# A trunk layer with a top-2 expert stage on one core: other order of the first loads, the first unit's weight homes freed by halves, the last unit's second matrices and its adding store by column halves

## The chip, the core and the metric

The kernel runs on one core of a Trainium2 chip. The time is the device time of the core in microseconds. Three runs of the kernel before took 1055.2, 1055.73 and 1056.48 us. Everything is float32.

## What is computed

One inference step of one trunk layer on 640 tokens (512 latent, 128 context) of width 1024:

```
mod = silu(cond) @ w_ada + b_ada                  # 6 x 1024 shifts, scales, gates; two conditions
h   = rmsnorm(x) * (1 + sc1) + sh1
x   = x + g1 * token_mixing(h)                    # Fourier, RG-LRU, short convolution, attention, merged by gates
h   = rmsnorm(x) * (1 + sc2) + sh2
x   = x + g2 * moe(h)                             # 32 experts, top-1 group of 8, top-2 in it
expert e: y = (silu(h @ w1[e]) * (h @ w3[e]) * weight) @ w2[e]     # 1024 -> 256 -> 1024
```

The change touches the very start (the first modulation chunks) and the expert stage.

## The kernel before

Each engine has its own instruction list, in an order written out by hand; semaphores tie them together. All loads of weights are issued by SyncE (the SP queue), one after another in that list, and land in about that order. GpSimd (POOL) issues the indirect transfers.

**Start.** `w_ada` comes in 12 chunks of 2 MB (`ada0` to `ada11`). TensorE turns each into a row of modulations (`modulation`, L812), ScalarE copies it out (`take_rows`, L1443), `modulation_T` (L823) turns two rows into columns, and VectorE makes shifts and scales of them (L1786 to L1802). Beside it the tokens `x0` (1.5 MB, three tiles) and `x1` (1 MB, two tiles) are squared on ScalarE (L1440), POOL makes the inverse norms, and VectorE scales the tokens (L1779). VectorE first waits for `consts` (the identity among them, L1768), since its list has that wait ahead of L1779. TensorE then transposes the tokens (`tokens_T`, L829), ScalarE and VectorE modulate them on their way out of PSUM (L1448, L1794), and the first input projection `zP0` (L867) begins; it also needs `win0`. Only chunks 0 and 2 are needed for that. `spin(n, 3)` (L835) issues n products of a block of ones whose result nobody reads; it stands ahead of chunk 0 (48) and between chunks 0 and 2 (14).

**Expert stage.** 17 units (0 to LAST = 16) of two experts each (unit 8 has one, for tokens beyond an expert's 64 rows). An expert's matrices are one block: W1 and W3 together (`w13`, 2 MB) and W2 (`w2`, 1 MB). There are NBUF = 6 homes, so that expert i+6 takes the home of expert i. For a unit u TensorE's list is: transpose its 128 gathered rows (`pair_T`, L1321), `hidden_of(u)` (L1328: 32 products over 8 blocks of rows, in two halves, and between them the transpose of the unit before), and `project` (L1344: 16 products). The order in the loop is `hidden_of(u+1)`, `pair_T(u+2)`, `project(u)`. When `hidden_of(u)` is done (`s_A`), SP issues the `w13` of the two experts that follow in those homes; when `project(u)` is done (`s_Y`), their `w2`. ScalarE and VectorE make the activation and, after the unit before has been scaled (`s_yd`), the gate rows for this one (`slot_g2`: L1706 on ScalarE, then L2395 on VectorE). VectorE multiplies the product with them, 512 columns at a time (L2405), and POOL adds the 128 rows to the output in HBM by one indirect transfer (`scatter`, L2632). POOL also gathers the rows of the units (L2628).

**Around unit 0** TensorE's list is: `second_gate_row(0)` (L1369), `hidden_of(0)`, `second_gate_row(1)`, `pair_T(1)`, the table of left-over tokens (L1382, 20 products into the same PSUM slot as the gate rows), then the loop, which begins with `hidden_of(1)`. ScalarE takes out of PSUM, in this order: the rows of unit 0 (L1683), both gate rows (L1693), the rows of unit 1.

**The last unit** has experts 31 and 32 of the stream. Before, SP issues their `w13` as the two lower halves, then the two upper halves (`w13_rest`), so that TensorE can begin on the lower halves; their `w2` comes last, whole.

Of the kernel before, what the change touches and what calls it, by code (L numbers as in the profile page):

```python
# [15 lines left out]
KD = D // P  # L16
# [145 lines left out]
W13_PIECES = [4 if 2 <= i < NBUF else 1 for i in range(len(STREAM))]  # L162
# [31 lines left out]
def build(nc, a, out):  # L194
    ctx = ExitStack()
    with ctx:
# [3 lines left out]
        def sem(name):  # L200
            return ctx.enter_context(nc.semaphore(name))
# [135 lines left out]
        xtab = sb("xtab", 3, I32)  # L337

# [128 lines left out]
        s_first = sem("first_unit_rows_chosen")  # L467
# [23 lines left out]
        w13_rest = sem("last_w13_upper_rows_loaded")  # L491
# [102 lines left out]
        def _(sp):  # L594
# [18 lines left out]
            load("cols", cols[:, :], a["cols"])  # L613
            load("x0", xtok[:, 0:3, :], x_dram[:, 0:3, :])
            load("x1", xtok[:, 3:TT, :], x_dram[:, 3:TT, :])
            ring("ada0", a["w_ada"][0])
            load("consts", consts[:, :], a["consts"])
            ring("ada2", a["w_ada"][2])
# [72 lines left out]

            for e in range(2):
                load_w13(e)
                load_w2(e)
# [53 lines left out]
            for u in range(LAST + 1):  # L748
                if u == 2:

                    sp.wait_ge(s_xtab, 2)
                    for h in range(2):
                        sp.dma_start(table_d[0:2 * XCOLS].rearrange("(c h) r k -> h r c k", h=2)[h], tab[h * C:(h + 1) * C, PAIRS:TCOLS, :]) \
                            .then_inc(s_over, 16)
                    sp.wait_ge(s_slot, 1)
                    e_x = sp.value_load(xinfo[0:1, 0:1], min_val=0, max_val=NE - 1)
                    n_x = sp.value_load(xinfo[0:1, XCH:XCH + 1], min_val=1, max_val=XCH)
                if AFTER[u]:
                    sp.wait_ge(s_A, u + 1)
                for i in AFTER[u]:  # L760
                    if i in AT[LAST]:
                        load_piece(i, wexp[i % NBUF][0][:, 0:W13 // 2], 0, W13 // 2, w13_loaded[i % NBUF])
                    else:
                        load_w13(i)
                for i in AFTER[u]:
                    if i in AT[LAST]:
                        load_piece(i, wexp[i % NBUF][0][:, W13 // 2:W13], W13 // 2, W13, w13_rest)
                if u and AFTER[u - 1]:
                    sp.wait_ge(s_Y, u)
                    for i in AFTER[u - 1]:  # L770
                        load_w2(i)
# [11 lines left out]
            sp.wait_ge(y_stored[0], 16 * (LAST // 2 + 1))  # L783
# [6 lines left out]
        def _(pe):  # L790
# [47 lines left out]
            spin(48, 3)  # L838
            pe.wait_ge(s_scond, 1)
            modulation(0)  # L840
            spin(14, 3)
# [496 lines left out]
            def project(halves, slot=2):  # L1338

                for n in range(2):  # L1340
                    for f in range(2):
                        for lo, homes, hid in halves:
                            w = homes[f] if len(homes) == 2 else homes[0][:, f * D:(f + 1) * D]
                            ins = mm(psum[lo:lo + C, slot, n * 512:(n + 1) * 512], hid[:, f, :],  # L1344
                                     w[:, n * 512:(n + 1) * 512], start=(f == 0), stop=(f == 1))
                return ins
# [5 lines left out]
            def hidden_of(u):  # L1352
                for i in AT[u]:
                    pe.wait_ge(w13_loaded[i % NBUF], 16 * pieces_until(W13_PIECES, i))
                pe.wait_ge(s_xTd, u + 1)
                halves = [(lo, wexp[i % NBUF][0], xgT[u % 2][:, :, lo:lo + C]) for lo, i in zip((0, C), AT[u])]
                hidden(H_SLOT[u % 2], halves, range(0, KD // 2))
                if u:
                    pe.wait_ge(s_hid, u)
                    hidden_T(H_SLOT[(u - 1) % 2], gate_e[:, (u - 1) % 2, :]).then_inc(s_hf, 1)  # L1360
                if u == LAST:
                    pe.wait_ge(w13_rest, 16 * len(AT[LAST]))
                hidden(H_SLOT[u % 2], halves, range(KD // 2, KD)).then_inc(s_A, 1)
# [7 lines left out]

            pe.wait_ge(s_lgd, TT)
            second_gate_row(0)
            pe.wait_ge(s_cntd, 2)
            hidden_of(0)
            pe.wait_ge(s_g2r, 1)
            second_gate_row(1)
            pair_T(1)
# [6 lines left out]
            for u in range(LAST + 1):  # L1385
# [10 lines left out]
                if u and u < LAST:  # L1396
                    pe.wait_ge(s_yd, u)
                pe.wait_ge(s_hT, u + 1)
                project([(lo, wexp[i % NBUF][1:], hT[:, u % 2, :, lo:lo + C]) for lo, i in zip((0, C), AT[u])], Y_SLOT[u]) \
                    .then_inc(s_Y, 1)  # L1400
# [24 lines left out]
        def _(act):  # L1425
# [265 lines left out]
            for i in range(2):  # L1691
                act.wait_ge(s_g2f, i + 1)
                A(g2_row[:, i, :], psum[:, 2, :], ACT.Copy).then_inc(s_g2r, 1)  # L1693
            take_pair_T(1)
            act.wait_ge(s_g2r, 2)
# [31 lines left out]
        def _(dve):  # L1727
# [603 lines left out]
            v.tensor_copy(pair_w[:, 0:PAIRS, :], filled_tab[:, :, 1:3]).then_inc(s_tab, 1)  # L2331

# [56 lines left out]
            for p in range(LAST + 1):  # L2389
# [14 lines left out]
                for n in range(2):  # L2404
                    ins = v.tensor_tensor(y_sb[:, p % 2, n * 512:(n + 1) * 512],  # L2405
                                          psum[:, Y_SLOT[p], n * 512:(n + 1) * 512], slot_g2[n], ALU.mult)
                ins.then_inc(s_yd, 1)
# [38 lines left out]
        def _(pool):  # L2446
# [191 lines left out]
            def put_rows(u):  # L2638
# [9 lines left out]
                scatter(y_sb[0:n, u % 2, :], tab[0:n, TAB_COL[u], 0:1], y_stored[u % 2])  # L2648
# [145 lines left out]
```

## Time and profile before

| | |
|---|---|
| median of three runs | 1055.73 us (1055.2 to 1056.48) |
| the profiled execution, its own time | 1053.14 us |
| its span from first to last instruction | 1051.3 us |
| PE, DVE, ACT, POOL busy | 94%, 49%, 22%, 25% of the span |
| mean granted TensorE clock | 0.977 of full |
| moved by DMA | 193.65 MB, 184 GB/s over the span |

A time stamp counts from the span's start. A busy share says how much an engine worked, not that it set the end: for that the chain of waits is read back from the last instruction, and in the expert stage the rate of the transfers in short windows.

### The profile page before, as it was taken

The numbers are of one execution on the slowest core, as the hardware profiler recorded it, in microseconds if no ns is written. First come the engines' busy times: TensorE is split into PE (matmuls) and PEld (weight loads), VectorE is DVE, ScalarE is ACT, GpSimd is POOL, SyncE is SP. The second block draws the span as 40 slices with busy tenths as digits, with TensorE's granted clock in tenths as the row PEclk, the third lists the DMA queues.
The fourth block names the chain that finished last, engine by engine and source line by source line (L and its number), as shares of the span: only waits on it lengthen the run. The fifth ranks groups of instructions, "written<-read, shape, count | busy, mean of one in ns | idle before, by whom it ended". The sixth has DMA issues, their size and how long they took to land.

```text
span 1051.3 us, 11753 instructions
## 1 busy us (share of the span) xinstructions
PE 992.0 (94%) x4332; PEld 590.7 (56%) x4332; DVE 516.0 (49%) x1018; ACT 232.9 (22%) x464; POOL 265.0 (25%) x268
## 2 busy tenths in 40 slices
PE   8899999999999999999999999999999998878785
PEld 6566656655555677777777777745584332322231
DVE  3378652255645345667667655537674321321223
ACT  3224330134555311111111111111112111211111
POOL 0333310011530133544465334200010211211101
PEclk9999999999999999999999999999989998998988
DMA  9735346000000271221311421275379999999995
GB/s 370 298 139 230 120 177 254 1 6 2 1 1 1 101 289 52 65 87 51 101 51 57 166 68 61 79 274 168 113 292 355 332 401 398 399 426 399 403 409 175
DMA packets 37625, 193.65 MB, mean 184 GB/s; under 512 B 7658, under 2 KB 12458, under 8 KB 27712
## 3 DMA queue, kind: packets, MB, share of 16 engines
q1 hardware_dynamic: 32800, 182.31, 45.1%
q0 software_dynamic: 4624, 10.06, 3.9%
q8 instruction: 35, 0.57, 0.2%
q10 hardware_dynamic: 144, 0.52, 0.1%
q14 instruction: 22, 0.18, 0.1%
HBM read 185.50 MB, written 14.09 MB: 190 GB/s over the span
## 4 chain that ended last, share of the span: by engine, by line
PE 79%; DMA 10%; SPq 3%; DVE 2%; issue 2%; ACT 2%; POOL 0%; POOLq 0%; DVEq 0%; ACTq 0%
PE psum L1110 23%; PE psum L867 8%; PE psum L1144 7%; PE psum L1186 7%; PE psum L1328 6%; DMA r_bv<-in_w_e 4%; PE psum L960 3%; PE psum L1344 3%; DMA r_w<-in_w_e 3%; PE psum L1044 3%; SPq L678 2%; PE psum L1060 2%; PE psum L812 2%; DMA r_w<-in_w_ada 2%; PE psum L1071 2%
## 5 line engine op out<-in xcount | busy, mean ns | idle before, releaser
L1110 PE MATMUL psum<-r_h,r_w 128*128 128x320 f32 x512 | 143.6, 433 | 0.0
L2604 POOL TENSOR_TENSOR r_w<-r_w 128x512 f32<-128x512 f32 x64 | 84.7, 1332 | 221.6 <-PE psum L1110 155.0
L1110 PEld LDWEIGHTS psum<-r_h,r_w 128*128 128x128 f32 x512 | 97.1, 190 | 40.6 <-issue 0.3
L1110 PE MATMUL psum<-r_ys,r_w 128*128 128x320 f32 x384 | 111.2, 432 | 0.0
L1110 PEld LDWEIGHTS psum<-r_ys,r_w 128*128 128x128 f32 x384 | 73.0, 190 | 30.4
L1613 ACT ACTIVATE r_bv<-r_bv 128x320 f32<-128x320 f32 x64 | 30.1, 470 | 238.8 <-DVE r_bv L2141 238.8
L2632 POOL DMA_INDIRECT out_y<-r_bv,tab x17 | 26.8, 1577 | 202.0 <-DVE r_bv L2405 202.0
L1186 PE MATMUL psum<-r_w,r_bv 128*128 128x512 f32 x160 | 72.2, 597 | 0.0
L2150 DVE TENSOR_TENSOR r_t<-psum,r_t 128x320 f32<-128x320 f32 x112 | 52.2, 483 | 9.3 <-PE psum L1144 8.0
L2127 DVE SCALAR_TENSOR_TENSOR r_t<-r_bv,r_t 128x320 f32<-128x320 f32 x48 | 46.8, 975 | 1.2 <-ACT r_bv L1613 1.2
L2141 DVE TENSOR_TENSOR sqbuf<-psum,r_bv 128x320 f32<-128x320 f32 x32 | 15.7, 492 | 64.4 <-PE psum L1110 64.4
L1687 ACT ACTIVATE r_t<-psum 128x256 f32<-128x256 f32 x17 | 6.5, 385 | 182.1 <-PE psum L1328 180.2
L1186 PEld LDWEIGHTS psum<-r_w,r_bv 128*128 128x128 f32 x160 | 29.2, 190 | 30.3 <-issue 30.3
L2385 DVE COPY r_t<-psum 128x256 f32<-128x256 f32 x17 | 7.2, 425 | 77.5 <-PE psum L1335 77.5
L2085 DVE TENSOR_REDUCE tinys<-psum 128x1 f32<-128x640 f32 (+1 forms) x40 | 28.6, 716 | 18.5 <-PE psum L1045 18.3
L1044 PE MATMUL psum<-r_a,r_bv 96*128 96x512 f32 x64 | 34.5, 620 | 2.5 <-ACT r_bv L1552 0.8
L2141 DVE TENSOR_TENSOR r_bv<-psum,r_bv 128x320 f32<-128x320 f32 x32 | 15.7, 491 | 41.8 <-PE psum L1110 41.7
L2136 DVE TENSOR_TENSOR r_bv<-r_bv,r_t 128x320 f32<-128x320 f32 x48 | 35.8, 746 | 0.4
L2378 DVE SCALAR_TENSOR_TENSOR r_t<-r_t,psum 128x256 f32<-128x256 f32 x17 | 7.2, 421 | 58.0 <-ACT r_t L1687 58.0
L1328 PE MATMUL psum<-r_c,r_ckv 128*64 128x512 f32 x64 | 30.3, 620 | 4.9 <-issue 4.9
L2454 POOL TENSOR_TENSOR tinys<-tinys 128x2 f32<-128x2 f32 (+2 forms) x11 | 7.6, 690 | 105.6 <-DVE tinys L2202 105.1
L2395 DVE SCALAR_TENSOR_TENSOR sqbuf<-r_d,tab,sqbuf 128x512 f32<-128x512 f32 x17 | 12.8, 751 | 35.0 <-ACT r_d L1706 35.0
(461 smaller groups left out, 2019.0 us busy)
## 6 DMA issues: line engine op xcount, KB each, us to landing
r_a<-in_w_ada SPq DMA_DIRECT2D x8, 2048.0 KB, 8.5
r_w<-in_w_gate SPq DMA_DIRECT2D x32, 512.0 KB, 4.6
r_a<-in_w_e SPq DMA_DIRECT2D x6, 2048.0 KB, 31.7
r_c<-in_w_e SPq DMA_DIRECT2D x5, 2048.0 KB, 31.2
r_c<-in_w_e SPq DMA_DIRECT2D x8, 1024.0 KB, 34.9
r_w<-in_w_e SPq DMA_DIRECT2D x4, 2048.0 KB, 34.3
r_ys<-in_w_e SPq DMA_DIRECT2D x4, 2048.0 KB, 36.4
r_bv<-in_w_e SPq DMA_DIRECT2D x4, 2048.0 KB, 36.6
```

Source lines behind the costliest of these rows:

```text
L867: ins = mm(dst, w_n[:, k, :], z_mix0[:, k // 2, k % 2, :] if n == 4 else x[:, k, :], start=(k == 0), stop=(k == HK - 1))
L960: mm(o[:, 0:512], x, w[:, 0:512], start=(k == 0), stop=(k == KD - 1))
L1044: mm(o[:, 0:NLAT], q, kT[0:QK, h, 0:NLAT], start=True, stop=True)
L1110: ins = mm(gate_bank(u, n), w[:, k, :], x[:, k, :], start=(k == 0), stop=(k == HK - 1))
L1144: ins = mm(branch_bank(u, seq), x_w[:, k, :], xs_[k], start=(k == 0), stop=(k == kb - 1))
L1186: ins = mm(out_bank(t, n), merged[:, k, tokens_of(t)], w[:, (k % 4) * D + n * 512:(k % 4) * D + (n + 1) * 512], start=(k == 0), stop=(k == ...
L1328: ins = mm(psum[lo:lo + C, slot, 0:2 * FE], xT[:, k, :], w[:, k * 2 * FE:(k + 1) * 2 * FE], start=(k == 0), stop=(k == KD - 1))
L1344: ins = mm(psum[lo:lo + C, slot, n * 512:(n + 1) * 512], hid[:, f, :], w[:, n * 512:(n + 1) * 512], start=(f == 0), stop=(f == 1))
L2127: v.scalar_tensor_tensor(out=merged[:, 2 * i + j, part] if b == 0 else bquad[n], in0=gth[:, j, part], scalar=1.0, in1=bquad[n], op0=ALU.ad ...
L2136: v.tensor_tensor(merged[:, 2 * i + j, part], merged[:, 2 * i + j, part], bquad[n], ALU.add) \
L2150: v.tensor_tensor(bsum[:, dst, :], branch_bank(u, seq), bsum[:, more, :], ALU.add).then_inc(s_badd, 1)
L2604: g.tensor_tensor(w_mix[n], x, y, op).then_inc(s_wm, 1)
```

## The change

Start: `ada0` is issued ahead of the tokens, and `ada2` ahead of `consts`. The products of ones are 22 ahead of chunk 0 and 44 between chunks 0 and 2.

Unit 0: its two homes are reloaded in halves. `s_first` counts once more when the lower half of `hidden_of(0)` is done; SP then issues the lower halves of experts 6 and 7, and the upper halves after `s_A`. In TensorE's list `hidden_of(0)` stands ahead of `second_gate_row(0)`, and `pair_T(1)` ahead of `second_gate_row(1)`; ScalarE's list follows.

Last unit: `w13` comes whole again. Its `w2` comes as 512 left columns of both experts, then 512 right columns. `project`, the scaling and the adding store go by these halves: two indirect stores of 128 rows x 512 columns, with row numbers `last_rows` of an output seen as 1280 rows of 512.

```diff
-W13_PIECES = [4 if 2 <= i < NBUF else 1 for i in range(len(STREAM))]
+W13_PIECES = [4 if 2 <= i < NBUF else 2 if i in (NBUF, NBUF + 1) else 1 for i in range(len(STREAM))]
...
+            ring("ada0", a["w_ada"][0])
             load("x0", xtok[:, 0:3, :], x_dram[:, 0:3, :])
             load("x1", xtok[:, 3:TT, :], x_dram[:, 3:TT, :])
-            ring("ada0", a["w_ada"][0])
+            ring("ada2", a["w_ada"][2])
             load("consts", consts[:, :], a["consts"])
-            ring("ada2", a["w_ada"][2])
             ring("win0", a["w_in"][0])
...
+            def load_w2_columns(i, n, done):
+                halves = lambda w: w.rearrange("p (f n) -> p f n", f=2)[:, :, n * 512:(n + 1) * 512]
+                sp.dma_start(halves(wexp[i % NBUF][1]), halves(a["w_e"][STREAM[i][1], :, W13:EW])).then_inc(done, 16)
...
+                if u == 0:
+                    sp.wait_ge(s_first, TT + 1)
+                    for i in AFTER[0]:
+                        load_w13(i, (0,))
                 if AFTER[u]:
                     sp.wait_ge(s_A, u + 1)
                 for i in AFTER[u]:
-                    if i in AT[LAST]:
-                        load_piece(i, wexp[i % NBUF][0][:, 0:W13 // 2], 0, W13 // 2, w13_loaded[i % NBUF])
+                    if u == 0:
+                        load_w13(i, (1,))
                     else:
                         load_w13(i)
-                for i in AFTER[u]:
-                    if i in AT[LAST]:
-                        load_piece(i, wexp[i % NBUF][0][:, W13 // 2:W13], W13 // 2, W13, w13_rest)
                 if u and AFTER[u - 1]:
                     sp.wait_ge(s_Y, u)
                     for i in AFTER[u - 1]:
-                        load_w2(i)
+                        if i not in AT[LAST]:
+                            load_w2(i)
+                    for n, done in enumerate((w2_loaded, [w2_rest] * NBUF)):
+                        for i in AFTER[u - 1]:
+                            if i in AT[LAST]:
+                                load_w2_columns(i, n, done[i % NBUF])
...
             pe.wait_ge(s_set, 1)
-            spin(48, 3)
+            spin(22, 3)
             pe.wait_ge(s_scond, 1)
             modulation(0)
-            spin(14, 3)
+            spin(44, 3)
             modulation(2)
...
-                hidden(H_SLOT[u % 2], halves, range(0, KD // 2))
+                ins = hidden(H_SLOT[u % 2], halves, range(0, KD // 2))
+                if u == 0:
+                    ins.then_inc(s_first, 1)
...
+            pe.wait_ge(s_cntd, 2)
+            hidden_of(0)
             pe.wait_ge(s_lgd, TT)
             second_gate_row(0)
-            pe.wait_ge(s_cntd, 2)
-            hidden_of(0)
+            pair_T(1)
             pe.wait_ge(s_g2r, 1)
             second_gate_row(1)
-            pair_T(1)
...
+                else:
+                    project(halves, Y_SLOT[u], (0,)).then_inc(s_Y, 1)
+                    pe.wait_ge(w2_rest, 16 * len(AT[LAST]))
+                    project(halves, Y_SLOT[u], (1,)).then_inc(s_Y, 1)
...
-            for i in range(2):
+            def take_second_gate_row(i):
                 act.wait_ge(s_g2f, i + 1)
                 A(g2_row[:, i, :], psum[:, 2, :], ACT.Copy).then_inc(s_g2r, 1)
+            take_second_gate_row(0)
             take_pair_T(1)
+            take_second_gate_row(1)
...
+            for h in range(2):
+                v.tensor_scalar(last_rows[:, h:h + 1], filled_tab[:, TAB_COL[LAST], 0:1], 2.0, h - 2.0, ALU.mult, ALU.add)
...
+                half_rows = out["y"].rearrange("t (h n) -> (t h) n", h=2)
+                for h in range(2):
+                    pool.wait_ge(s_yd, u + 1 + h)
+                    pool.indirect_dma_start(half_rows, bass.IndirectOffsetOnAxis(ap=last_rows[:, h:h + 1], axis=0),
+                                            y_sb[:, u % 2, h * 512:(h + 1) * 512], None, bounds_check=2 * NT - 1,
+                                            oob_is_err=False, compute_op=ALU.add).then_inc(y_stored[u % 2], 16)
```

## Rows read from the trace of the kernel before

**Rows 1.** Page, DMA busy share in tenths, 40 slices of 26.3 us.

```profile
DMA  9735346000000271221311421275379999999995
```

**Rows 2.** Chain that ended last, the start: start us, us, what.

```profile
3.81 19.45 DMA r_w<-in_w_ada
...
32.06 4.54 PE psum L867 x16
```

**Rows 3.** Timeline, the start: start us, us, engine, line [idle before <- releaser].

```profile
1.44 13.30 PE L835 MATMUL psum<-ones 128*128 128x128 f32 x96 [1.44 <-DVE ones L1732]
...
16.11 1.92 PE L812 MATMUL psum<-r_w,scond 128*32 128x512 f32 x16 [1.37 <-DMA r_w<-in_w_ada]
...
17.38 0.08 DVE L1768 MEMSET tinys<- 128x30 f32 x1 [8.69 <-DMA consts<-in_consts]
...
17.83 3.39 DVE L1779 TENSOR_SCALAR r_a<-r_a,tinys 128x1024 f32<-128x1024 f32 x5
...
17.96 3.39 PE L835 MATMUL psum<-ones 128*128 128x128 f32 x28
...
23.30 3.61 PE L812 MATMUL psum<-r_w,scond 128*32 128x512 f32 x16 [1.95 <-DMA r_w<-in_w_ada]
...
28.23 2.50 POOL L2482 TENSOR_TENSOR r_a<-r_ys 128x512 f32<-128x512 f32 x2 [12.01 <-DMA r_ys<-in_w_in]
...
28.59 2.35 PE L829 MATMUL psum<-consts,r_a 128*128 128x128 f32 x20
...
29.57 1.18 DVE L1802 SCALAR_TENSOR_TENSOR mod<-ada,cols 128x8 f32<-128x8 f32 x1
```

**Rows 4.** Windows, the start: us, busy of each engine (count), TensorE clock, DMA share, GB/s.

```profile
23.40:26.80 3.40, 3.40 (x16) 0.49 (x15) 0.00 (x0) 0.00 (x0) 0.00 (x0) 0.50 1.04 443
```

**Rows 5.** Windows of the expert stage.

```profile
794.00:797.00 3.00, 3.00 (x24) 2.30 (x21) 0.83 (x2) 0.34 (x1) 0.00 (x0) 1.00 0.72 213
...
806.00:810.00 4.00, 4.00 (x24) 1.64 (x22) 0.84 (x2) 1.57 (x3) 0.00 (x0) 1.00 0.51 140
...
836.00:1033.00 197.00, 165.65 (x708) 58.48 (x706) 49.80 (x88) 31.52 (x48) 31.88 (x24) 0.92 1.02 405
```

**Rows 6.** Chain that ended last, TensorE around unit 0.

```profile
785.65 1.98 PE psum L1369 x16
787.63 7.02 PE psum L1328 x32
...
797.83 2.39 PE psum L1382 x20
```

**Rows 7.** Timeline around unit 0: ScalarE's copy, SP's issue.

```profile
785.63 1.02 ACT L1683 ACTIVATE r_ckv<-psum 128x1024 f32<-128x1024 f32 x1 [8.70 <-PE psum L1233]
...
807.80 0.33 SPq L678 DMA_DIRECT2D r_w<-in_w_e  x1
```

**Rows 8.** Chain that ended last, the end.

```profile
1038.30 3.67 PE psum L1344 x16
```

**Rows 9.** DMA issued at 991.99 us (last w13 piece): KB, us to landing.

```profile
r_w<-in_w_e SPq DMA_DIRECT2D x1, 1024.0 KB, 35.1
```

**Rows 10.** Timeline, the end.

```profile
1025.65 0.59 PE L1328 MATMUL psum<-r_c,r_ckv 128*64 128x512 f32 x1
...
1038.30 0.61 PE L1344 MATMUL psum<-r_c,r_t 128*64 128x512 f32 x1 [1.29 <-DMA r_w<-in_w_e]
...
1038.80 0.72 ACT L1706 ACTIVATE sqbuf<-r_d,tab 128x512 f32<-128x512 f32 x1 [3.94 <-DVE r_bv L2405]
...
1040.84 0.74 DVE L2395 SCALAR_TENSOR_TENSOR r_d<-r_d,tab 128x512 f32<-128x512 f32 x1
...
1042.66 0.68 DVE L2405 TENSOR_TENSOR r_bv<-psum,r_d 128x512 f32<-128x512 f32 x1
...
1044.13 1.55 POOL L2632 DMA_INDIRECT out_y<-r_bv,tab  x1 [3.02 <-DVE r_bv L2405]
```

**Rows 11.** DMA issued at 1044.13 us (last adding store): us to landing.

```profile
out_y<-r_bv,tab POOLq DMA_INDIRECT x1, 5.6
```

More of the change, by code:

```diff
@@ L337, in build @@
         xtab = sb("xtab", 3, I32)
+        last_rows = sb("last_rows", 2, I32)
         R = {}
@@ L466, in build @@
         s_h2d = sem("h2_stored")
-        s_first = sem("first_unit_rows_chosen")
+        s_first = sem("first_unit_rows_chosen_and_low_half_projected")
         s_g2f, s_g2r = sem("second_gate_rows_filled"), sem("second_gate_rows_ready")
@@ L490, in build @@
         w13_loaded = [sem(f"w13_loaded{i}") for i in range(NBUF)]
-        w13_rest = sem("last_w13_upper_rows_loaded")
+        w2_rest = sem("last_w2_upper_columns_loaded")
         w2_loaded = [sem(f"w2_loaded{i}") for i in range(NBUF)]
@@ L782, in _ @@
             overflow(sp, n_x, load_chunk)
-            sp.wait_ge(y_stored[0], 16 * (LAST // 2 + 1))
+            sp.wait_ge(y_stored[0], 16 * (LAST // 2 + 2))
             sp.wait_ge(y_stored[1], 16 * (LAST // 2))
@@ L1336, in hidden_T, with project @@
                 return ins
-            def project(halves, slot=2):
-                for n in range(2):
+            def project(halves, slot=2, ns=range(2)):
+                for n in ns:
                     for f in range(2):
@@ L1360, in hidden_of @@
                     hidden_T(H_SLOT[(u - 1) % 2], gate_e[:, (u - 1) % 2, :]).then_inc(s_hf, 1)
-                if u == LAST:
-                    pe.wait_ge(w13_rest, 16 * len(AT[LAST]))
                 hidden(H_SLOT[u % 2], halves, range(KD // 2, KD)).then_inc(s_A, 1)
@@ L1398, in _ @@
                 pe.wait_ge(s_hT, u + 1)
-                project([(lo, wexp[i % NBUF][1:], hT[:, u % 2, :, lo:lo + C]) for lo, i in zip((0, C), AT[u])], Y_SLOT[u]) \
-                    .then_inc(s_Y, 1)
+                halves = [(lo, wexp[i % NBUF][1:], hT[:, u % 2, :, lo:lo + C]) for lo, i in zip((0, C), AT[u])]
+                if u < LAST:
+                    project(halves, Y_SLOT[u]).then_inc(s_Y, 1)
+                else:
+                    project(halves, Y_SLOT[u], (0,)).then_inc(s_Y, 1)
+                    pe.wait_ge(w2_rest, 16 * len(AT[LAST]))
+                    project(halves, Y_SLOT[u], (1,)).then_inc(s_Y, 1)
                 if u == 2:
@@ L2404, in _ @@
                 for n in range(2):
+                    if p == LAST:
+                        dve.wait_ge(s_Y, p + 1 + n)
                     ins = v.tensor_tensor(y_sb[:, p % 2, n * 512:(n + 1) * 512],
                                           psum[:, Y_SLOT[p], n * 512:(n + 1) * 512], slot_g2[n], ALU.mult)
-                ins.then_inc(s_yd, 1)
+                    if n or p == LAST:
+                        ins.then_inc(s_yd, 1)
                 if p != LAST - 2:
@@ L2647, in put_rows @@
                 n = rows_of(u)
-                scatter(y_sb[0:n, u % 2, :], tab[0:n, TAB_COL[u], 0:1], y_stored[u % 2])
+                if u < LAST:
+                    scatter(y_sb[0:n, u % 2, :], tab[0:n, TAB_COL[u], 0:1], y_stored[u % 2])
+                    return
+                half_rows = out["y"].rearrange("t (h n) -> (t h) n", h=2)
[4 more added lines that the diff above has]
+                                            oob_is_err=False, compute_op=ALU.add).then_inc(y_stored[u % 2], 16)
             pool.wait_ge(s_wo, 2 * TT)
```

## The prediction

> **What bounds the kernel now.** I read the digits of the DMA share first: high in the first slices, low through the middle, 9 to the end from slice 30 on [rows 1]. So three regimes: a start fed by loads, a long middle with few transfers, and an expert stage with full transfers. Then the chain of waits, start and end, tells which wait ends last in each.
>
> Start: the chain is the landing of `ada2` at 23.26 (3.81 + 19.45), its product, the column transposes, the modulation of the tokens, and `zP0` at 32.06 [rows 2]. The timeline shows the loads landing in issue order: `ada0` at 16.1, `consts` at 17.4, `ada2` at 23.3, `win0` at 28.2, and that the tokens are scaled (L1779) from 17.83, right after `consts`, long before they are wanted at 28.59 [rows 3]. The product of chunk 2 runs at the low clock, 0.50 granted or 1.2 GHz, and takes 3.61 us instead of 1.92 [rows 3, 4].
>
> Expert stage: from 836 to 1033 the DMA share is 1.02 at 405 GB/s while TensorE is busy 165.65 of 197 us [rows 5]. TensorE waits for weights, not weights for TensorE. The stream has two holes ahead of that: 794 to 797 (213 GB/s) and 806 to 810 (140 GB/s) [rows 5]. Against 405 that is 3 x 192 / 405 = 1.4 us and 4 x 265 / 405 = 2.6 us of lost transfer. The first is the wait for unit 0's homes, the second ends with the reload issued at 807.80, which is the end of `hidden_of(1)` [rows 7]. End: last `w2` landed just before 1038.30, 16 products until 1041.97, scaling until 1043.34, store issued at 1044.13 and landed 5.6 later at 1049.7 [rows 8, 10, 11].
>
> **Part 1, the start.** No byte is added. `ada0` gets ahead of 2.5 MB of tokens; at 4.9 us per 2 MB (`ada2` to `win0`, 28.2 - 23.3) it lands 6.1 us earlier, at 10.0. `ada2` gets ahead of `consts` (17.4 - 16.1 = 1.3 us): 22.0. `consts` closes the same sum of bytes as `ada2` did: 23.3. `win0` stays at 28.2 [rows 3].
> The products of ones: the first 48 took 13.30 us (slow at first), the next 14 took 3.39, or 0.24 each; so 22 end near 9, and 44 after chunk 0's product (10.0 + 1.9 = 11.9) take some 10 and end at 22. The product of chunk 2 then runs without an idle gap at the high clock until 23.9, and ScalarE's copy and the column transposes (before: from 26.91 to 28.59, 1.7 us) are done at 25.6. That is 3.0 us earlier than before.
> But `consts` is now late: VectorE's list goes from 17.38 to 23.3, and the scaled tokens come at 23.3 + 0.45 + 3.39 = 27.2 instead of 21.2 [rows 3]. The token transposes wait for all five: 27.2 instead of 28.59. VectorE's shifts and scales are queued behind the tokens in its own list. Before, the last of these small operations took 1.18 us, beside POOL's mixing of `win0` (28.23 to 30.7) [rows 3]; now they come ahead of it and are estimated at 0.6 together, so done at 27.8, in time for the first transposed block. Four blocks of transposes take 2.35, so `zP0` starts at 29.6, after `win0` (28.2). Gain 32.06 - 29.6 = **2.4 us**. What follows is TensorE's own chain, and the next loads are not earlier but had room; so the gain is kept until the expert stage.
> Bounds: up to 3.0, if only the modulation chain counts; 1.4, if the small operations stay as long (27.2 + 32.06 - 28.59 = 30.7); down to 0.9, if the idle gap of 1.6 us between the column and the token transposes costs the high clock. The trace has a gap of 1.37 us after which the product took 1.92, and one of 1.95 after which it took 3.61 [rows 3, 4]. I take the first, as the nearer one; the second is a stretch of 3.4 us at half speed, of which about 1.5 lie on the path (the rest under the wait for VectorE).
>
> **Part 2, unit 0.** SP issues two lower halves once half of `hidden_of(0)` is done. That list is TensorE's, so the order counts. Before: gate row 1.98, hidden 7.02 (until 794.65), gate row again 1.98, 1.2 until the table, filled by `pair_T(1)` (1.1), table 2.39, `hidden_of(1)` at 800.22 [rows 6]. After:
> - `hidden_of(0)` needs ScalarE's copy of its rows, 785.63 to 786.65; the first gate row covered that. It now starts at 786.7 and ends at 793.7, 0.9 earlier; its half is done at 790.2.
> - gate row 0 until 795.7; ScalarE copies it (1.0) under `pair_T(1)`, until 796.8.
> - gate row 1 until 798.8. `pair_T(1)` used to cover its copy. Now nothing does: ScalarE is done at 799.9.
> - table until 802.3. `hidden_of(1)` starts **2.1 us later** than before, and so do its end (809.9), the issue of experts 8 and 9, and the restart of the stream.
> The lower halves are in the queue at 790.3, the older loads last until 794.6, so the first hole is filled: 1.4 us. But the 4 MB then end at about 805, and the second hole reaches from there until the reload after `hidden_of(1)`. Since nothing is left in the queue then, all later bytes start 2.1 us later, behind a stream that is full until 1033. Cost **+2.1 us**. Bounds: if the restart were not what counts, the filled hole would give -1.4; if the new idle times of 1.1 us (785.6 and 798.8) took the clock down, one stretch of 3.4 us at half speed as in [rows 4] adds up to 1.7: +3.8.
>
> **Part 3, the last unit.** The bytes are the same, the last piece lands at 1038.2 as before (relative to the stream). What changes is who waits for what:
> - `hidden_of(LAST)` started at 1025.65 on the lower halves [rows 10]; the upper half of expert 32 landed at 991.99 + 35.1 = 1027.1 [rows 9]. Now both whole blocks are needed at the start: TensorE begins up to 1.4 us later.
> - TensorE before stood 1.29 us idle ahead of the last product, so its delay is hidden there. But the gate rows are not: ScalarE begins them when the unit before is scaled, 1038.80, and VectorE is done with them at 1041.6 [rows 10], 0.4 ahead of the product's end. 1.4 later they are ready at 1043.0, and VectorE's two halves end at 1043.7 and 1044.4 (before: 1043.34 the second).
> - POOL issues two stores, 1.55 each and some 0.3 between. First at 1043.7 + 0.8 = 1044.5, second at 1046.3 instead of 1044.13 [rows 10]. Half the rows' bytes are left for it: landing after 5.6 if the size does not matter, after 2.8 if it all does [rows 11]. I take 4.6, since the 1.55 of issue come first in it and do not shrink. It lands at 1050.9 instead of 1049.7: **+1.2 us**.
> Bounds: -0.8 (no delay of `hidden_of(LAST)`, second store landing in 4.0), +2.3 (size of the store without effect).
> The Trainium skill bears on this place: "DMA: Bandwidth & Descriptors", section "Anatomy of one DMA", gives a transfer issued by GpSimd about 2 us fixed and the rest as bytes over 436 GB/s, so that halving a store of 0.5 MB would save an estimated 0.6 us. By it alone the second store lands in 5.0 and the part costs 1.6. It speaks against splitting a store whose issue is serial.
> `last_rows` adds two small VectorE operations beside idle time; the `w2` column halves are 2 KB runs instead of 8 KB, taken at nothing (up to 0.4).
>
> **Sum.** -2.4 + 2.1 + 1.2 = +0.9 on the profiled 1053.14 (1051.3 and 1.8 around it): 1054.0. The median of the runs is 2.6 above the profiled one; the forecast for the median is 1055.73 + 0.9 = **1056.6 us**.
>
> **Rivals.**
> - A, the forecast, +0.9. Chance 0.42.
> - B, the filled hole counts and the later restart does not. For it: TensorE is idle 31 us of the 197 later on [rows 5], so its lateness at one unit might drown. Against: the queue is empty at the restart. -2.4 - 1.4 + 1.2 = -2.6, 1053.1 us. Chance 0.28.
> - C, slower: the start's new idle gap of 1.6 us ahead of the token transposes takes the clock down, place L829 and `zP0`, price 1.5 of the 2.4. It decides from a gap between 1.37 (kept) and 1.95 (lost). +0.9 + 1.5 = +2.4, 1058.1 us. Chance 0.20.
> - D, the new order of loads does not do what it says, since `consts` or chunk 0 lands later than worked out and the chain is no shorter than before: +3.3, 1059.0 us. Chance 0.10.
>
> What a measurement of this kernel can tell from no change is 0.2%, 2.1 us: below 1053.6 is faster, above 1057.8 slower. B lies just below, C just above, A in the middle. Faster: most of B and an edge of A, 0.25. Slower: most of C, D, 0.23. Same 0.52. The range that holds 8 in 10 goes from half a microsecond beyond B to half one beyond C: 1052.5 to 1058.7; A's own is 1054.8 to 1058.
>
> **What would show it.** Start: L812's second group at 22 and 1.92 long; L1768 at 23.3; L829 near 27.2; `zP0` near 29.6. Unit 0: ScalarE's second L1693 ends right ahead of L1382; `hidden_of(1)` 2 us later against the end of L1233; 794 to 797 at full rate, and a longer hole until the reload of experts 8 and 9. End: first L1328 of the last unit waits for r_w; the two L2632 stand 1.8 apart, and the second lands under 5.6. I am wrong if the span from the reload of experts 8 and 9 to the last `w2` landing gets shorter by more than 1 us, or if the holes of 794 to 810 lose less than 4 us in all.

## The result, and the profile after

The changed kernel takes 1062.66 us (median of 5, 1060.67 to 1064.47) beside 1055.20 for the kernel before on the same chip: ratio 1.0065, 95% interval [1.0045, 1.0085]. It is 6.9 us slower, where 0.9 was forecast, and outside the range given. The profiled execution took 1063.33 us with a span of 1061.3; before it was 1053.14 with 1051.3, an execution 2.1 to 2.6 below its medians. So the two profiles lie 10.0 apart and the medians 7.5.

In the changed kernel `hidden` is L1339, the gate rows L1380, the table L1393, `pair_T` L1332, `project` L1355. The chain of waits around unit 0 (start us, us, what) answers to [rows 6]:

```profile
785.94 1.03 ACT r_ckv L1699
...
787.10 7.09 PE psum L1339 x32
794.19 1.99 PE psum L1380 x16
...
796.21 1.03 ACT r_d L1709
...
797.28 2.06 PE psum L1380 x16
...
799.37 1.03 ACT r_d L1709
...
800.54 3.15 PE psum L1393 x20
803.69 6.13 PE psum L1339 x16
...
810.19 3.58 PE psum L1339 x16
```

The order is as worked out: second gate row, ScalarE's copy on the path, table. But the table takes 3.15 instead of 2.39, and the first 16 products of `hidden_of(1)` take 6.13 where the next 16 of the same form take 3.58. The windows of the expert stage (us, busy of PE, PEld, DVE, ACT, POOL with counts, TensorE clock, DMA share, GB/s) say why:

```profile
794.00:797.00 3.00, 3.00 (x26) 2.72 (x24) 1.14 (x2) 0.79 (x1) 0.00 (x0) 1.00 1.05 423
802.00:808.80 6.80, 6.80 (x23) 3.02 (x24) 1.10 (x4) 0.38 (x1) 0.00 (x0) 0.50 0.54 223
806.00:810.00 4.00, 4.00 (x14) 1.04 (x10) 0.00 (x0) 0.00 (x0) 0.00 (x0) 0.65 0.02 10
810.00:814.00 4.00, 4.00 (x21) 1.36 (x20) 0.42 (x1) 0.18 (x1) 0.00 (x0) 1.00 0.00 0
...
1034.00:1037.50 3.50, 3.50 (x10) 1.29 (x12) 0.00 (x0) 0.00 (x0) 1.03 (x1) 0.51 1.03 402
```

The clock stood at 0.50, 1.2 GHz, for 6.8 us of uninterrupted products. What TensorE did before it fell is in the timeline. It stood idle under ScalarE's copies, 1.14 us ahead of `hidden_of(0)` and 1.21 us ahead of the table:

```profile
787.10 0.61 PE L1339 MATMUL psum<-r_a,r_ckv 128*64 128x512 f32 x1 [1.14 <-ACT r_ckv L1699]
...
800.54 3.15 PE L1393 MATMUL psum<-r_bv,r_t 128*128 128x30 f32 x20 [1.21 <-ACT r_d L1709]
```

The clock fell at 802.0, 1.5 us after the second of them had ended and 14.9 after the first. The first hole of the stream is filled (423 GB/s, before 213 [rows 5]), the second is 8 us of nearly nothing (10 and 0 GB/s). It ends with the reload of experts 8 and 9:

```profile
790.79 0.33 SPq L679 DMA_DIRECT2D r_a<-in_w_e  x1
...
813.81 0.33 SPq L679 DMA_DIRECT2D r_w<-in_w_e  x1
```

That is 6.0 later than before [rows 7]. The start, in the chain:

```profile
4.46 18.71 DMA consts<-in_consts
...
23.77 3.33 DVE r_a L1798 x5
...
27.14 4.04 PE psum L840 x20
31.18 4.31 PE psum L878 x16
```

`zP0` (L878) starts 0.9 earlier than at 32.06 [rows 2]. The end, in the timeline:

```profile
1033.95 0.98 PE L1339 MATMUL psum<-r_c,r_ckv 128*64 128x512 f32 x1 [2.86 <-issue]
...
1048.84 0.72 ACT L1725 ACTIVATE sqbuf<-r_d,tab 128x512 f32<-128x512 f32 x1 [3.94 <-DVE r_bv L2428]
...
1053.72 1.55 POOL L2678 DMA_INDIRECT out_y<-r_bv,last_rows  x1 [2.56 <-DVE r_bv L2428]
1055.58 1.55 POOL L2678 DMA_INDIRECT out_y<-r_bv,last_rows  x1 [0.30 <-issue]
```

DMAs issued at 1027.85 (the last piece of `w2`) and at 1055.58 (the second store), us to landing:

```profile
r_w<-in_w_e SPq DMA_DIRECT2D x1, 512.0 KB, 17.3
...
out_y<-r_bv,last_rows POOLq DMA_INDIRECT x1, 4.0
```

The last weight is there at 1045.2, the last store at 1059.6. Before, [rows 8, 11] put them at 1038.2 and 1049.7: the tail grew from 11.5 to 14.4 us.

**The account.** Four lengths between events that every trace shows, in us. Stage: SP's first issue of the expert stage. Reload: from there to the issue of experts 8 and 9. Stream: from there to the last landing of `w2`. Late: from there until ScalarE begins the last gate rows, which is when unit 15 has been scaled. Chain: from there to the landing of the last store.

| kernel | stage | reload | stream | late | chain |
|---|---|---|---|---|---|
| before | 768.0 | 39.8 | 230.4 | 0.6 | 10.9 |
| changed | 768.3 | 45.5 | 231.4 | 3.7 | 10.8 |
| e1 start only | 766.6 | 38.9 | 230.1 | 0.1 | 11.3 |
| e2 unit 0 only | 768.1 | 45.5 | 230.6 | 0.0 | 11.2 |
| e3 last only | 768.1 | 40.4 | 230.4 | 3.7 | 11.0 |
| e4 unit 0, filled | 768.3 | 42.2 | 230.1 | 0.0 | 12.9 |
| e5 halves only | 769.9 | 38.9 | 231.0 | 2.7 | 10.3 |
| e6 order only | 765.5 | 44.6 | 231.2 | 2.7 | 10.3 |
| e7 whole w13 only | 768.6 | 39.9 | 230.6 | 3.6 | 10.4 |
| e8 unit 1 first | 767.4 | 35.8 | 233.3 | 0.1 | 11.2 |
| e9 last, filled | 766.8 | 39.8 | 230.5 | 2.0 | 10.9 |
| e10 last, w13 by halves | 765.5 | 39.9 | 230.6 | 2.4 | 10.8 |
| e11 start, filled | 767.8 | 38.9 | 230.8 | 2.4 | 10.2 |
| e12 all, filled | 767.0 | 41.3 | 230.8 | 2.2 | 10.8 |
| e13 unit 1 first + start | 766.7 | 35.8 | 231.2 | 2.4 | 10.3 |

Of the 9.9 us between the two profiles, 0.3 lie ahead of the stage, 5.7 in unit 0, 1.0 in the stream and 2.9 in the tail. The table also warns of what one execution is worth. Kernels with an unchanged start reach the stage at 765.5 to 769.9. With an unchanged last unit the tail (late and chain) is 11.2 to 11.5 four times (before, e1, e2, e8) and 12.7 to 13.0 five times (e4, e5, e6, e11, e13), and these five are the ones in which the clock fell to 0.50 for 3.4 us while the last two units' products ran (at 1028.5 to 1041.0).

The reload column holds 0.9 us of such chance too. In all fifteen profiles the clock falls once between 768 and 776 us, ahead of unit 0, for 6.8 us in eight of them and for 3.4 in seven, and from the stage's first issue to SP's issue of the two loads into `r_bv` (785.59 in the kernel before, 785.89 in the changed one) it takes 17.6 to 18.2 us in the eight and 16.7 in the seven. Counted from that issue, the reload depends on the order and the fillers alone, to 0.02 us:

| TensorE's order around unit 0 | kernels | us to the reload |
|---|---|---|
| as before | before, e1, e3, e5, e7, e9, e10, e11 | 22.2 |
| the change's, idle times open | changed, e2, e6 | 27.9 |
| the change's, idle times filled | e4, e12 | 24.6 |
| unit 1 ahead of the table | e8, e13 | 19.1 |

### The profile page after: what moved, and what is told of

The parts are those of the page before. It is cut to its first block, busy times and chain, and to the rows that moved or that the text cites. A ratio compares the mean times of both kernels' runs of the same rounds, so it can differ in the third digit from the quotient of the medians.

```text
span 1061.3 us, 11776 instructions
## 1 busy us (share of the span) xinstructions
PE 999.3 (94%) x4340; PEld 596.9 (56%) x4340; DVE 515.0 (49%) x1020; ACT 232.8 (22%) x464; POOL 266.3 (25%) x269
## 3 DMA queue, kind: packets, MB, share of 16 engines
q1 hardware_dynamic: 33600, 182.31, 44.6%
## 4 chain that ended last, share of the span: by engine, by line
PE 86%; issue 4%; DMA 4%; DVE 3%; ACT 2%; POOL 1%; SPq 0%; POOLq 0%; ACTq 0%; DVEq 0%
PE psum L1121 23%; PE psum L1339 12%; PE psum L878 8%; PE psum L1155 7%; PE psum L1197 7%; PE psum L1355 5%; PE psum L971 3%; PE psum L1055 3%; PE psum L1071 2%; DMA consts<-in_consts 2%; DMA r_w<-h_scratch,tab 2%; PE psum L1082 2%; PE psum L1000 2%; PE psum L823 2%; PE psum L1332 1%
## 5 line engine op out<-in xcount | busy, mean ns | idle before, releaser
L1339 PE MATMUL psum<-r_c,r_ckv 128*64 128x512 f32 x64 | 32.2, 655 | 7.1 <-issue 7.1
L2104 DVE TENSOR_REDUCE tinys<-psum 128x1 f32<-128x640 f32 (+1 forms) x40 | 28.7, 717 | 19.1 <-PE psum L1056 19.0
L2155 DVE TENSOR_TENSOR r_bv<-r_bv,r_t 128x320 f32<-128x320 f32 x48 | 35.8, 746 | 0.4
L1339 PE MATMUL psum<-r_h,lruw 128*64 128x512 f32 x48 | 25.0, 669 | 6.6 <-issue 6.6
```

The lines of the kernel that those rows point to most:

```text
L1339: ins = mm(psum[lo:lo + C, slot, 0:2 * FE], xT[:, k, :], w[:, k * 2 * FE:(k + 1) * 2 * FE], start=(k == 0), stop=(k == KD - 1))
L2155: v.tensor_tensor(merged[:, 2 * i + j, part], merged[:, 2 * i + j, part], bquad[n], ALU.add) \
```

## Experiments

All are timed against the kernel before in 5 rounds; "us" beside a ratio is its distance from 1, times 1055, and intervals in us are made the same way.

**e1, the start alone.**

```diff
+            ring("ada0", a["w_ada"][0])
             load("x0", ...)
             load("x1", ...)
-            ring("ada0", a["w_ada"][0])
-            load("consts", consts[:, :], a["consts"])
             ring("ada2", a["w_ada"][2])
+            load("consts", consts[:, :], a["consts"])
...
-            spin(48, 3)
+            spin(22, 3)
...
-            spin(14, 3)
+            spin(44, 3)
```

> The kernel before with the start part alone. Theory 1 (each part costs by itself): zP0 begins at 31.2 as in the changed kernel, 0.9 us earlier than before, because the clock falls in the idle gap ahead of the token transposes; the time is 0.9 below the kernel before (-1.5 to 0 after other clock drops). Rival: the new order shifts something later and the start costs time by itself: +1 us or more.

Measured 0.9998 [0.9983, 1.0014]: no gain. In its profile `zP0` starts at 30.54, but another way than in the changed kernel: a fall of the clock at 11.3 stretched the products of ones, so that chunk 2 ran at 23.8, not 22. Ahead of that fall TensorE had waited 2.24 us for chunk 0, since the 22 products of ones had ended at 8.0. The same stands in e11, e12 and e13: idle 2.19 to 2.44, a fall at 11.3 to 11.6, chunk 2 at 23.8 to 24.0. In the changed kernel the wait was 1.29 us, and no fall followed there.

**e2, unit 0 alone** (lower halves and order; its edit is that of e5 and e6 together).

> The kernel before with the unit-0 part alone (halves, and the new order of TensorE and ScalarE). Theory 1: the reload of experts 8 and 9 is issued 5 to 6 us later against the first SP issue of the stage, the last w2 lands as much later, the time is +5 to +6.5 us. Rival (the loss sits in the last unit, the later restart is absorbed): +0 to +1.

Measured 1.0054 [1.0033, 1.0074], 5.7 us. The half-speed stretch is there as in the changed kernel, 801.7 to 808.6. So most of the loss is this part's.

**e3, the last unit alone** (whole `w13`, `w2` by column halves, split store).

> The kernel before with the last-unit part alone. Theory 1: from the last w2 landing to the last store landing 14.4 us instead of 11.5, so +2.9 us (+1.2 if the clock happens to stay up at the start of the last unit). Rival (the tail is only long in the changed kernel because the stream is later): 11.5 as before, +0.

Measured 1.0032 [1.0010, 1.0053], 3.4 us; late 3.7.

**e4, unit 0 with its gaps filled.** Products of ones, whose result nobody reads, at the two places where TensorE newly waits.

```diff
+            pe.wait_ge(s_htd, 2 * TT)
+            spin(5, 3)
             pe.wait_ge(s_cntd, 2)
             hidden_of(0)
...
             second_gate_row(1)
+            spin(5, 3)
             pe.wait_ge(s_xsel, 1)
```

> As the unit-0 part alone, with 5 products of ones in each of TensorE's two new waits (ahead of hidden_of(0) and ahead of the table). Theory 1a (2.1 us are the order's, 3.3 the clock's): the clock stays at 1.00 through hidden_of(1), reload of experts 8 and 9 some 2.1 to 2.6 us later than before instead of 5.7, time +2 to +3. Rival (the clock falls for another reason, or all of it is the order): reload and time as with the unit-0 part alone, +5 to +6.5.

Measured 1.0019 [1.0000, 1.0038], 2.0 us: 3.7 less than e2. The chain, and the window of the stretch:

```profile
786.01 1.20 PE psum L841 x10
787.21 7.03 PE psum L1334 x32
...
799.38 1.31 PE psum L841 x10
800.69 2.28 PE psum L1393 x20
802.97 3.58 PE psum L1334 x16
```

```profile
802.00:808.80 6.80, 6.80 (x37) 2.90 (x38) 1.52 (x5) 0.38 (x1) 0.00 (x0) 1.00 0.60 246
```

`hidden_of(1)` (L1334 here) takes 3.58 for its first half, and the reload comes 42.2 after the stage's first issue instead of 45.5. The table still starts as late as in the changed kernel. So 2.4 are the order's (24.6 - 22.2 in the second table), 3.3 the clock's (27.9 - 24.6).

**e5, the lower halves alone.**

```diff
+                if u == 0:
+                    sp.wait_ge(s_first, TT + 1)
+                    for i in AFTER[0]:
+                        load_w13(i, (0,))
...
+                    elif u == 0:
+                        load_w13(i, (1,))
                     else:
                         load_w13(i)
```

> The kernel before with unit 0's homes given back by halves, TensorE's and ScalarE's order as before. Theory 2 (only the restart counts, the issue of experts 8 and 9 after hidden_of(1)): the hole at 794 to 797 is filled, the second hole grows by as much, the reload of experts 8 and 9 stays 13 us behind the upper half of expert 6 (39.8 after the stage's first issue), time within 1 us of before. Rival (filled hole counts): last w2 landing 1.4 us earlier, time -1.4.

Measured 1.0007 [0.9985, 1.0030]. The first hole is filled, and the second stays (the stage begins 1.9 later here than before, 769.9):

```profile
794.00:797.00 3.00, 3.00 (x21) 1.74 (x18) 1.80 (x3) 0.00 (x0) 0.00 (x0) 1.00 1.05 417
...
806.00:810.00 4.00, 4.00 (x24) 1.75 (x22) 0.78 (x2) 0.60 (x2) 0.00 (x0) 1.00 0.50 154
```

Before, they were 213 and 140 GB/s [rows 5]. A filled hole ahead of an empty queue brought no time that can be measured. The interval alone, -1.6 to +3.2 us, would just hold the -1.4 of the forecast's rival B. The trace decides: the reload is no earlier (22.2 as before), and the stream behind it is no shorter (231.0, before 230.4).

**e6, the order alone.**

```diff
-            pe.wait_ge(s_lgd, TT)
-            second_gate_row(0)
             pe.wait_ge(s_cntd, 2)
             hidden_of(0)
+            pe.wait_ge(s_lgd, TT)
+            second_gate_row(0)
+            pair_T(1)
             pe.wait_ge(s_g2r, 1)
             second_gate_row(1)
-            pair_T(1)
```

> The kernel before with the new order of TensorE and ScalarE around unit 0 alone, homes given back whole. Theory 2: all of the unit-0 loss is the order's: reload of experts 8 and 9 some 45.5 us after the stage's first issue (39.8 before), time +5 to +6. Rival (the halves have a price of their own, in more pieces or a fuller queue): clearly less than the +5.7 of the unit-0 part as a whole.

Measured 1.0068 [1.0044, 1.0091], 7.1 us: as much as the whole change. Table 3.63, `hidden_of(1)` 5.63 for its first half: the stretch again, this time from 797.8.

**e7, whole `w13` blocks in the last unit alone.**

```diff
                 for i in AFTER[u]:
-                    if i in AT[LAST]:
-                        load_piece(... lower rows ...)
-                    else:
-                        load_w13(i)
-                ... upper rows, w13_rest ...
+                    load_w13(i)
...
-                if u == LAST:
-                    pe.wait_ge(w13_rest, 16 * len(AT[LAST]))
```

> The kernel before with the last unit's w13 loaded whole, w2 and the store whole as before. Theory 3 (the tail's loss is the wait of hidden_of(LAST) for the whole w13, with the clock falling in it): TensorE idle 2.5 to 3 us ahead of the last unit, clock 0.50 after it, last w2 landing to last store landing 14 to 14.5 us, time +2.5 to +3. Rival (the split store, two issues in a row on POOL, is the loss): 11.5 as before, time +0.

Measured 1.0024 [1.0003, 1.0045], 2.5 us of e3's 3.4. TensorE waits 4.34 us for the second block and starts at the low clock:

```profile
1028.09 1.08 PE L1322 MATMUL psum<-r_c,r_ckv 128*64 128x512 f32 x1 [4.34 <-issue]
```

**e8, unit 1 projected ahead of the table.** The other way round: since the restart of the stream counts, the work that only feeds the overflow table goes behind `hidden_of(1)`.

```diff
             hidden_of(0)
+            pair_T(1)
             pe.wait_ge(s_g2r, 1)
             second_gate_row(1)
-            pair_T(1)
+            hidden_of_1()
...
-                if u < LAST:
+                if 0 < u < LAST:
                     hidden_of(u + 1)
...
+                if u == 0:
+                    pe.wait_ge(s_hid, 1)
+                    hidden_T(H_SLOT[0], gate_e[:, 0, :]).then_inc(s_hf, 1)
```

> The kernel before with unit 1 projected (both halves in one go) ahead of the table of left-over tokens, so that its homes come free some 3 us earlier; unit 0's activation then waits for the table. Theory 2: reload of experts 8 and 9 some 37 us after the stage's first issue instead of 39.8, the second hole all but gone, last w2 landing 2.5 to 3 us earlier, time -2 to -3. Rival (TensorE's own list sets the pace here, and it gets a wait of some 2 us for unit 0's activation): time +0 to +2.

Measured 0.9973 [0.9953, 0.9994], 2.8 us faster than the kernel before. The chain has no idle time until the table is taken:

```profile
786.09 7.02 PE psum L1328 x32
793.11 1.02 PE psum L1321 x8
794.13 1.98 PE psum L1376 x16
796.11 7.02 PE psum L1328 x32
803.12 2.36 PE psum L1390 x20
```

The reload comes 4.0 earlier, 3.1 by the order (19.1 instead of 22.2) and 0.9 by the shorter stretch near 771. The stream gives 2.9 back (233.3 instead of 230.4): unit 0's second product, 6.42 long at half speed from 808.57, releases homes late (a reading of the trace, not tried by itself). In e13 the same order gave 231.2.

**e9, the last unit with its gap filled.**

```diff
             def hidden_of(u):
+                if u == LAST:
+                    spin(12, H_SLOT[u % 2])
```

> Last unit's part alone, as in e3, with 12 products of ones ahead of hidden_of(LAST), in the idle time of 2.6 to 4.3 us in which TensorE waits there for whole w13 blocks. Theory (the wait costs twice, by its length and by the half-speed stretch of 3.4 us that follows it, and what it delays is the gate rows' chain that ends the kernel): no half-speed stretch in hidden_of(LAST), so its second half ends 1.5 to 1.9 us earlier against the landing of its blocks, and from the last w2 landing to the last store's landing 14.7 falls to 12.8 to 13.2; time 1.5 to 1.8 below e3, 1.0015 of before. Rival (the tail's length is the two serial stores and the columns, TensorE's lateness is hidden): the tail stays at 14 to 14.7 and the ratio at 1.003.

Measured 1.0022 [1.0000, 1.0043], 1.1 less than e3, which the intervals don't separate. In the profile no stretch follows, and late is 2.0 instead of 3.7:

```profile
1021.40 2.94 PE L839 MATMUL psum<-ones 128*128 128x128 f32 x24
...
1025.82 0.61 PE L1332 MATMUL psum<-r_c,r_ckv 128*64 128x512 f32 x1 [1.48 <-issue]
```

**e10, the last unit with `w13` by halves as before**, so `w2` by column halves and the split store alone.

> Last unit's part alone, but with w13 by halves of the rows as before; w2 by column halves and two stores of half rows stay. Theory (the whole w13 blocks are what costs): hidden_of(LAST) starts 1 to 1.5 us earlier than in e3 and without a long wait, the tail from the last w2 landing is 10.7 to 12.3 (before 11.5), ratio 0.999 to 1.001. Rival (two serial stores of half rows cost by themselves, since POOL issues them one after the other): tail 12.5 or more, ratio 1.001 to 1.003.

Measured 0.9999 [0.9977, 1.0021]. The time is as the theory had it. The profile isn't: a tail of 13.3, since here a gap of 2.59 us ahead of `project` of unit 15 was followed by a half-speed stretch from 1031.4. That such tails occur with an unchanged last unit too, after such a stretch (12.7 to 13.0, above), leaves the parts' worth in this experiment to the ratio: nothing that can be measured. The split store shows in the last length: where the gate rows end last (late 2.0 or more), chain is 10.8 to 11.0 with the two stores (changed, e3, e9, e10, e12) and 10.2 to 10.4 with one (e5, e6, e7, e11, e13). So it costs about 0.5 there. Where the gate rows are early, no run prices it.

**e11, the start with its gap filled.**

```diff
             modulation_T("ada_a0", (0, 2))
+            spin(6, 3)
```

> Start's part alone with 6 products of ones between the column transposes and the token transposes, in the idle gap ahead of L829. Theory (rival C of the forecast: the gap takes the clock down, and that is why zP0 comes 1.5 late): token transposes take 2.35 instead of 4.04, zP0 starts near 29.6 instead of 31.0, ratio 0.9978 (2.3 us faster). Rival (the start's gain is lost later, in stages that wait for other loads): zP0 near 29.6 and the ratio still 0.999 to 1.000. Second rival (the gap isn't the cause): zP0 stays at 30.5 to 31.

Measured 0.9993 [0.9971, 1.0016]. `zP0` came at 31.77, later even than the second rival had it. But this is no test of the gap. After the fall at 11.6 the column transposes came so late that there was none: in e1, without a filler, the token transposes began at 27.41 right behind them and took 2.35. Here the filler held them until 28.85. The timeline shows what bounds `zP0` now:

```profile
27.51 1.50 PE L835 MATMUL psum<-ones 128*128 128x128 f32 x12
27.72 0.23 DVE L1787 TENSOR_REDUCE adasum<-psum 128x16 f32<-128x64 f32 x1 [0.85 <-PE psum L823]
27.94 2.50 POOL L2483 TENSOR_TENSOR r_a<-r_ys 128x512 f32<-128x512 f32 x2 [6.09 <-DMA r_ys<-in_w_in]
27.98 1.26 DVE L1789 TENSOR_TENSOR ada<-adasum,cols 128x16 f32<-128x16 f32 x1
...
28.85 2.35 PE L829 MATMUL psum<-consts,r_a 128*128 128x128 f32 x20
29.27 1.19 DVE L1803 SCALAR_TENSOR_TENSOR mod<-ada,cols 128x8 f32<-128x8 f32 x1
...
31.77 0.51 PE L868 MATMUL psum<-r_h,r_ys 128*128 128x320 f32 x1 [0.57 <-ACT r_h L1450]
```

The transposes take 2.35, as in e1. But two small VectorE operations take 1.26 and 1.19, each about as long as one of POOL's two.

**e12, the whole change with all gaps filled** (the fillers of e4, e9 and e11 together).

> The whole change with products of ones in each idle gap that was seen to bring the clock down: 6 ahead of the token transposes, 5 ahead of hidden_of(0), 5 ahead of the table, 12 ahead of hidden_of(LAST). Theory (the time that the forecast lacks is the clock's: half-speed stretches behind short gaps in hidden_of(1) and hidden_of(LAST), and what is left is the later restart and the two waits, near what the steps gave): no half-speed stretch at 802 to 809 nor at 1034; reload of experts 8 and 9 42.2 after the stage's first issue (45.5 in the change), tail from the last w2 landing 12.9 (14.4 in the change); together 4.8 below the change, ratio to before 1.0015 to 1.0025. Rival (the clock falls elsewhere instead, or the fillers cost what they save): ratio 1.004 or more.

Measured 1.0015 [0.9995, 1.0035], 1.6 us, where the change without them measured 6.9. The tail is 12.9, as expected. The reload is 41.3 where 42.2 was expected; the 0.9 are the shorter stretch near 771, and from the `r_bv` issue it is 24.6, as in e4. There is no half-speed stretch at 802 to 809 or 1030 to 1038. The intervals of the two ratios do not meet. At the start there was no gap to fill, as in e11, so what the fillers gave is unit 0's and the last unit's.

**e13, e8's order with the change's order of the first loads.**

> Unit 1 projected whole ahead of the left-over table, as in e8, with the change's order of the first loads, as in e1; nothing of the change's other parts. Theory (they act in different stages, and both leave the end as it is): the reload of experts 8 and 9 35.8 after the stage's first issue, the stage's first issue 0.5 to 1.5 earlier than before, tail 11.3; ratio 0.997 to 0.9962, below both kernels. Rival (a start's gain is lost by the expert stage, and nothing adds to e8): 0.9973 to 0.998. Second rival (e8's gain was chance): 0.999 to 1.001.

Measured 0.9968 [0.9949, 0.9986], 3.4 us faster than the kernel before, the fastest of all here. Against e8's 0.9973 the start's share, 0.5 us, is below what can be told.

## Why the prediction was wrong

The direction of the sum was right and its size was not. **The step that failed is Part 2's term for the clock**, the largest of three misses. The forecast saw the two new idle times of 1.1 us and bounded what they could do at "one stretch of 3.4 us at half speed", 1.7, and left it out of the sum. It happened in all three profiled kernels with that order unfilled (changed, e2, e6), and in neither with it filled (e4, e12). The stretch was 6.8 us, twice the one of [rows 4], and all of it lay on the path to the reload: 3.3 by the second table (27.9 - 24.6), 3.7 by the ratios of e2 and e4. Together with the order, Part 2 measured 5.7 (e2) where 2.1 stood in the sum. The start measured -0.2 (e1, interval -1.8 to +1.5) where -2.4 stood, the last unit +3.4 (e3, interval +1.1 to +5.6) where +1.2 stood; both are taken up below. The bound of 1.7 was taken from one fall, and the trace of the kernel before holds longer ones. These are windows of it (columns as above):

```profile
771.00:777.60 6.60, 6.60 (x32) 6.60 (x33) 5.89 (x25) 0.59 (x3) 2.30 (x2) 0.50 1.03 367
880.20:886.80 6.60, 5.33 (x14) 1.86 (x16) 0.00 (x0) 0.00 (x0) 1.10 (x2) 0.50 1.05 394
```

and this its timeline ahead of the first:

```profile
769.48 0.66 PE L1198 MATMUL psum<-consts,r_h 128*128 128x128 f32 x4 [0.25 <-DVE r_h L2195]
770.82 1.87 PE L1207 MATMUL psum<-r_krr,r_t 128*128 128x36 f32 x8 [0.69 <-ACT r_t L1642]
```

In the first TensorE is busy all the time at 0.50, behind idle times of 0.25 and 0.69 among small products. That is the same length and a similar place as at unit 0, where small products (gate rows of 64x128, `pair_T`) stand ahead of the second gap. That the small products matter is a reading and was not tried. Read before the prediction, this stretch would have set the bound for one fall at 3.4, not 1.7.

- **Order, +2.1.** Right: 2.4 by the second table. In the changed kernel `hidden_of(0)` started at 787.1 and the table at 800.5, against 786.7 and 799.9 in the forecast. That the restart governs is shown too: over the thirteen kernels whose reload lay between 38.9 and 45.5, the stream behind it took 230.1 to 231.4, and the later reload was never made up.
- **First hole.** Filled as forecast, worth nothing (e5). The test that the forecast set itself, that the holes lose less than 4 us in all, did not come true: the second hole alone lost about 8 us.
- **Last unit, +1.2.** Right in the mechanism and near in size, if like is compared with like. Without a half-speed stretch at the end the tail is 11.2 to 11.5 with the last unit unchanged and 12.9 with whole blocks (e9, e12). With one it is 12.7 to 13.0 and 14.0 to 14.7 (e7, changed, e3). That is some 1.5 us both times. What the term lacks is the clock again: a wait ahead of `hidden_of(LAST)` that grew from nothing to 2.6 (e3), 2.9 (changed) and 4.3 us (e7) was followed by 3.4 us at half speed in all three. Since the kernel with an unchanged last unit has such a stretch in five of nine profiles too, of the tail's +2.9 only about 1.5 can be put down to the change. By ratios the part cost 3.4 [1.1, 5.6], too wide to tell the two apart.
- **The store's size.** The second half lands 4.0 after its issue, and 4.0 to 4.3 in e3, e9, e10 and e12; I took 4.6. The last whole store took 5.6 [rows 11], and 5.3 to 5.4 in the nine other kernels that have it. The estimate from the Trainium skill, "DMA: Bandwidth & Descriptors", section "Anatomy of one DMA", was 5.0; by the trace half the bytes saved 1.0 to 1.6, not the estimated 0.6. The second issue (1.86 behind the first) costs more than that, so the split doesn't pay: by about 0.5 in the chain where the gate rows end last.
- **Start, -2.4.** Chunk 0 landed at 10.3, chunk 2 ran at 22.3, `consts` came at 23.2, the transposes began at 27.1, each within 0.3 of the forecast. Then they took 4.04 instead of 2.35 behind an idle time of 1.09, shorter than the 1.37 of [rows 3] after which nothing was lost: rival C's mechanism, though not its condition, seen in this one profile and not tested. What Part 1 had at nothing is the wait ahead of chunk 0: it let the first 22 products end near 9 and chunk 0 land at 10.0, without a price for the idle time between. In four of the five profiles with the new start the clock fell behind that wait and put chunk 2 at 23.8 to 24.0 (e1, above). In e11 the two small operations, which in the changed kernel ran at 27.25 and 27.46 in 0.18 and 0.17, ahead of POOL's mixing, then fell beside it. The Trainium skill, "SBUF — State Buffer", section "Who interferes with whom", says that a VectorE instruction with two inputs in SBUF contends with a GpSimd instruction that reads SBUF; the trace agrees: they took 1.26 and 1.19 beside two POOL instructions of 1.25, while in the kernel before a reduction of one input, beside POOL's mixing too (28.79), took 0.23. In the five kernels with the new start `zP0` comes 0.3 to 1.5 earlier, and neither e1 nor e11 nor e13 against e8 tells the gain from nothing. What became of it between `zP0` and the expert stage isn't settled: half-speed stretches in attention fall differently in each execution (the changed kernel has one at 276, the kernel before none there), and they move the stage's start by more than the gain.

Chances: the forecast saw the clock as a risk at two places, the start's gap and unit 0's, gave a chance to the first alone (rival C, 0.20), and did not see it at the last unit at all. In the changed kernel's profile it fell at all three. Filled, the whole change measured 1.6, near the 0.9 of the sum, and 5.3 less than unfilled. That nearness is in part luck: the start's -0.2, the order's 2.4 and the last unit's 1.5 would make 3.7, the edge of its interval (-0.5 to 3.7). What is open: the parts alone sum to -0.2 + 5.7 + 3.4 = 8.9, the whole is 6.9, within the intervals; and which of unit 0's two gaps brings the clock down was not tried.

## What to carry to other kernels

Before an edit puts a wait of about a microsecond between short products, price it twice: as the wait, and as the products behind it at half speed, on the path or not. A run with a few products on ones in the gap tells the two apart. And where a queue runs empty and is full from its restart to the end, as here, the moment of the restart is what counts: look for what can be put behind the instruction that restarts it, here the table behind `hidden_of(1)`, worth 2.8 us (e8, interval 0.6 to 5.0), rather than for holes ahead of it. Before two profiles are compared length by length, count their half-speed stretches: with nothing changed, a longer one was worth 0.9 us ahead of unit 0, and one more some 1.5 us at the end.

## What the runs showed of the hardware

- The clock stood at 0.50 for 6.8 us though TensorE was busy from end to end, at 802 in the changed kernel and at 771 in the kernel before; others, as [rows 4], lasted 3.4. Near 771, behind the same instructions, it was 6.8 in eight profiles and 3.4 in seven.
- Idle 1.09 us was followed by a half-speed stretch at the start, idle 1.37 [rows 3] and 1.48 (e9) by none: the length of the gap alone doesn't decide.
- The last indirect adding store landed in 4.0 to 4.3 us with half rows, in 5.3 to 5.6 with whole rows, and two in a row are issued 1.86 apart on POOL.
- A VectorE operation of 8 or 16 elements a row with two inputs in SBUF took 0.17 to 0.18 us alone, and 1.13 to 1.26 where it began within 0.2 us after a POOL operation of 1.25 on SBUF.
